# Moving the context's load, transposes and squares from the boundary of two blocks into the feed forward before it

## The reference

```
x = first_block(x, mem, ...)          # per layer: mixer, memory cross attention, feed forward
# second block, layer 0
mod_x, mod_c = silu(c) @ ada_w + ada_b, silu(c_ctx) @ ada_w + ada_b
hx = rmsnorm(x,   n1_g) * (1 + sc1)  + sh1
hc = rmsnorm(ctx, n1_g) * (1 + csc1) + csh1
mx, mc = hybrid_mixer(hx, hc, w_in, ...)

def squared_relu_mlp(h, w1, w2):      # 1024 -> 4096 -> 1024
    a = relu(h @ w1)
    return (a * a) @ w2
```

## Time and profile before

| | |
|---|---|
| median of three runs | 3759.76 us |
| lowest, highest | 3759.74, 3764.34 us |
| the profiled execution | 3764.54 us |
| its span | 3762.7 us |
| PE busy | 3543.3 us, 94% of the span |
| DVE busy | 2017.1 us, 54% |
| ACT busy | 1232.1 us, 33% |
| mean granted clock of PE | 0.951 |

### The profile page before, as it was taken

The page is one execution under the profiler, slowest core; times in us unless marked ns, Lnnn a source line. Parts: engine busy times, 40 slices in busy tenths (PEclk is TensorE's granted clock), DMA queues, the critical chain, the costliest instruction groups (busy, mean ns, idle before and its releaser), DMA issues.

```text
span 3762.7 us, 42305 instructions
## 1 busy us (share of the span) xinstructions
PE 3543.3 (94%) x17448; PEld 2805.7 (75%) x17448; DVE 2017.1 (54%) x3717; ACT 1232.1 (33%) x2053; POOL 212.6 (6%) x302
## 2 busy tenths in 40 slices
PE   7999899999989999998999989999998998879998
PEld 6657678887867678887986557888887885558886
DVE  5565588856654588854126664323235236654344
ACT  4353343234453333233112222332233212134332
POOL 0200000001040000000000001000001000000000
PEclk9999999999999999999999859999999998789999
DMA  4302155522202145533210011212122220112331
GB/s 164 115 12 79 45 168 179 167 91 84 74 27 78 45 157 172 168 119 124 81 57 27 26 38 46 79 57 68 57 66 86 99 68 17 40 45 90 101 91 67
DMA packets 214108, 317.01 MB, mean 84 GB/s; under 512 B 5304, under 2 KB 162618, under 8 KB 212636
## 3 DMA queue, kind: packets, MB, share of 16 engines
q1 hardware_dynamic: 198108, 243.00, 19.9%
q0 software_dynamic: 15808, 71.31, 5.6%
HBM read 300.66 MB, written 14.49 MB: 84 GB/s over the span
## 4 chain that ended last, share of the span: by engine, by line
PE 83%; DVE 11%; ACT 4%; issue 2%; DMA 1%; POOL 0%; SPq 0%; DVEq 0%; ACTq 0%; POOLq 0%
PE ps L94 82%; DVE t L115 5%; ACT t L100 3%; DVE t L107 3%; PE ps L97 1%; DVE t L111 1%; DVE ps L107 0%; DVE ps L115 0%; DVE t L121 0%; DVE t L112 0%; DMA t<-gates_away 0%; DVE t L125 0%; DVE ps L112 0%; DVE t L118 0%; DMA t<-in_mem 0%
## 5 line engine op out<-in xcount | busy, mean ns | idle before, releaser
L94 PE MATMUL ps<-t,t 128*128 128x512 f32 (+7 forms) x17032 | 3486.5, 368 | 193.5 <-DVE t L107 98.1
L94 PEld LDWEIGHTS ps<-t,t 128*128 128x128 f32 (+3 forms) x17032 | 2753.2, 191 | 900.4 <-issue 177.3
L100 ACT ACTIVATE t<-t 128x1024 fp32r<-128x1024 f32 (+6 forms) x1168 | 831.0, 744 | 1226.7 <-PE ps L94 653.5
L107 DVE TENSOR_TENSOR t<-t,t 128x1024 fp32r<-128x1024 f32 (+5 forms) x882 | 781.7, 911 | 708.9 <-ACT t L100 693.5
L100 ACT ACTIVATE t<-ps 128x512 f32<-128x512 f32 (+5 forms) x490 | 248.5, 531 | 1062.7 <-PE ps L94 1027.7
L115 DVE SCALAR_TENSOR_TENSOR t<-t,t,t 128x256 f32<-128x256 f32 (+4 forms) x935 | 438.7, 530 | 7.6 <-ACT t L100 1.2
L107 DVE TENSOR_TENSOR t<-ps,t 128x512 f32<-128x512 f32 (+4 forms) x293 | 187.4, 659 | 248.2 <-PE ps L94 181.8
L115 DVE SCALAR_TENSOR_TENSOR t<-ps,t,t 128x512 f32<-128x512 f32 (+1 forms) x228 | 139.7, 662 | 279.7 <-PE ps L94 259.6
L107 POOL TENSOR_TENSOR t<-t,t 128x64 f32<-128x64 f32 (+1 forms) x196 | 129.3, 684 | 1724.9 <-ACT t L100 1721.6
L118 DVE COPY t<-ps 128x256 f32<-128x256 f32 (+3 forms) x169 | 75.9, 477 | 276.8 <-PE ps L94 256.7
L100 ACT ACTIVATE t<-ps,t 128x512 f32<-128x512 f32 (+3 forms) x106 | 61.6, 582 | 131.9 <-PE ps L94 94.6
(11 more groups left out here) (31 smaller groups left out, 293.3 us busy)
## 6 DMA issues: line engine op xcount, KB each, us to landing
t<-in_w_ff SPq DMA_DIRECT2D x64, 1024.0 KB, 7.6
t<-in_w_mlp SPq DMA_DIRECT2D x64, 1024.0 KB, 5.4
t<-in_ada_w POOLq DMA_DIRECT2D x48, 1024.0 KB, 5.9
t<-in_w_in SPq DMA_DIRECT2D x30, 1024.0 KB, 5.3
t<-in_w_qkv_o SPq DMA_DIRECT2D x12, 1024.0 KB, 5.1
t<-in_w_mem_kv SPq DMA_DIRECT2D x8, 1024.0 KB, 6.0
t<-in_w_mem_q SPq DMA_DIRECT2D x8, 1024.0 KB, 5.1
t<-in_w_mem_o SPq DMA_DIRECT2D x8, 1024.0 KB, 5.1
```

The lines of the kernel that those rows point to most:

```text
L94: return Issued(self, self.e and self.e.matmul(o, l, r, start=start, stop=stop, skip_group_check=True))
L100: return Issued(self, self.e and self.e.activation(o, i, f, **kw))
L107: return Issued(self, self.e and self.e.tensor_tensor(o, a, b, op))
```

## The change

The loading of `ctx_2` moves on SP's queue from the end of the last feed forward to the beginning of the first block's second feed forward, ahead of the load of its second weight block, into a buffer `FF1.CIN` that the stage leaves free; it waits for the last `pv` of the memory attention. In steps 6 to 13 PE transposes one chunk a step into bank 5, behind the step's matmuls, and ACT (even) or DVE (odd) copies it out in the same step. In steps 14 to 21 ACT squares one chunk a step, into the `SQ` buffers, and PE adds it up in bank 5, behind the step's matmuls and ahead of the modulation's. On ACT `context()` stands at the end of each step's work: in an `up` step behind relu, square and copy of both tiles. The norm reads bank 5 in place of 7.

```diff
--- before.py
+++ after.py
@@ -438,11 +438,10 @@
         if with_ada:
             f.ADA = [ar([128, 2048]) for _ in range(2)]
             f.ACC = [ar([128, 2, 256]) for _ in range(2)]
+            f.CIN = [ar([128, D]) for _ in range(2)]
         return f
 
     FF1, FF2 = ff_area(S, True), ff_area(S + C, False)
-    ar = Area(D1)
-    CIN = [ar([128, D]) for _ in range(2)]
     T = S + C
     ar = Area(D1)
     H = Tiles()
@@ -690,9 +689,24 @@
             f1, f2 = ff
             step = [0]
 
+            def context(s):
+
+                if s in range(6, 14):
+                    k = s - 6
+                    opening(5)
+                    pe.wait_ge("ctx_in", 1)
+                    for i in range(2):
+                        ins = pe.transpose(P[5][:, 128 * i:128 * i + 128], tiles.CIN[i][:, 128 * k:128 * k + 128], cst("ident"))
+                    ins.then_inc("ctxT", k)
+                    free[5] = [("ctxT_out", k)]
+                elif s in range(14, 22):
+                    square_sum(("n1_0", 1), 5, C, [s - 14], SQ)
+
             def modulate():
                 s = step[0]
                 step[0] += 1
+                if l == 1:
+                    context(s)
                 if l is None or s > 24 or s == 0:
                     return
                 pe.wait_ge("macc", l, s - 1, 1)
@@ -950,15 +964,6 @@
         memory_attention(1)
 
 
-        pe.wait_ge("ctx_in", 1)
-        for k in range(8):
-            bk = k % 4
-            opening(bk)
-            for i in range(2):
-                ins = pe.transpose(P[bk][:, 128 * i:128 * i + 128], CIN[i][:, 128 * k:128 * k + 128], cst("ident"))
-            ins.then_inc("ctxT", k)
-            free[bk] = [("ctxT_out", k)]
-        square_sum(("n1_0", 1), 7, C, range(8), TMP)
         for l in range(2):
             hybrid_tensor(pe, l, feature, tokens, square_sum, opening, free, normed, project_out, feed_forward)
 
@@ -1320,9 +1325,18 @@
                     for s, (dst, n) in enumerate(streams):
                         square_of(key, s, dst, n, m, ("ev", u.n, m, s))
 
-        def feed_forward(ff, tiles, nkey, key, segs, streams):
+        def feed_forward(ff, tiles, nkey, key, segs, streams, with_context=False):
             f1, f2 = ff
-            at_t = [0]
+            at_t, step = [0], [0]
+
+            def context():
+                s = step[0]
+                step[0] += 1
+                if with_context and s in range(6, 14, 2):
+                    act.wait_ge("ctxT", s - 6)
+                    act.activation(CX[:, s - 6, :], P[5][:, 0:C], ACT.Copy).then_inc("ctxT_out", s - 6)
+                elif with_context and s in range(14, 22):
+                    squares_of(("n1_0", 1), SQ, CX, C, [s - 14], lambda k: ("ctxT_out", k))
 
             def up(j):
                 for u in f1[j]:
@@ -1344,6 +1358,7 @@
                             act.wait_ge("sqr", key, j, t.m, z)
                             act.activation(hid, tb, ACT.Copy).then_inc("hidden_hi", key, j, t.m, z)
                             tmp_free[x] = ("hidden", key, j, t.m, z)
+                    context()
 
             tmp_free = {x: ("nlo", nkey, 7, len(streams) - 1) for x in range(2)}
             up(0)
@@ -1484,7 +1500,7 @@
                       MA.SB, MA.PT, lambda h, part: None)
             project_out(U.mo[l], f"ff{l}", [(X, S)])
             norm(f"ff{l}", [(P[6], S, 0, None)], HR1, [whole(U.mo[l][3])])
-            feed_forward(U.ff[l], FF1, f"ff{l}", "mix1" if l == 0 else "n1_0", [S], [(X, S)])
+            feed_forward(U.ff[l], FF1, f"ff{l}", "mix1" if l == 0 else "n1_0", [S], [(X, S)], l == 1)
 
         memory_attention(0)
 
@@ -1537,11 +1553,6 @@
         memory_attention(1)
 
 
-        for k in range(0, 8, 2):
-            act.wait_ge("ctxT", k)
-            act.wait_ge("pv", ("xat", 1), 3, 1)
-            act.activation(CX[:, k, :], P[k % 4][:, 0:C], ACT.Copy).then_inc("ctxT_out", k)
-        squares_of(("n1_0", 1), TMP, CX, C, range(8), lambda k: ("ctxT_out", k))
         for l in range(2):
             hybrid_scalar(act, l, start, square, sq_free, rs_free, roots, norm, project_out, feed_forward)
 
@@ -1554,7 +1565,7 @@
     def hybrid_scalar(act, l, start, square, sq_free, rs_free, roots, norm, project_out, feed_forward):
         nkey, segs, tasks = f"n1_{l}", segs_of(l), ret_tasks(l)
         hr_free = [whole(U.ff[1][1][7][1]) if l == 0 else whole(U.ff2[0][1][7][1])]
-        norm(nkey, [(P[6], S, 0, lambda k: MOD[l][:, k, 0:1]), (P[7], C, S, lambda k: MOD[l][:, k, 1:2])], HR2, hr_free)
+        norm(nkey, [(P[6], S, 0, lambda k: MOD[l][:, k, 0:1]), (P[5 if l == 0 else 7], C, S, lambda k: MOD[l][:, k, 1:2])], HR2, hr_free)
         for us, dst in ((U.rg[l], H.Q), (U.gg[l], H.K)):
             for u in us:
                 start(u)
@@ -1842,10 +1853,17 @@
             step = [0]
             at_t = [0]
 
+            def context(s):
+                if s in range(7, 14, 2):
+                    dve.wait_ge("ctxT", s - 6)
+                    dve.tensor_copy(CX[:, s - 6, :], P[5][:, 0:C]).then_inc("ctxT_out", s - 6)
+
             def modulate():
 
                 s = step[0]
                 step[0] += 1
+                if l == 1:
+                    context(s)
                 if l is None or s > 24:
                     return
                 if s > 0:
@@ -2114,10 +2132,6 @@
         memory_attention(1)
 
 
-        for k in range(1, 8, 2):
-            dve.wait_ge("ctxT", k)
-            dve.wait_ge("pv", ("xat", 1), 3, 1)
-            dve.tensor_copy(CX[:, k, :], P[k % 4][:, 0:C]).then_inc("ctxT_out", k)
         for l in range(2):
             hybrid_vector(dve, l, start, newton, norm, project_out, feed_forward)
 
@@ -2164,7 +2178,7 @@
             dve.wait_ge("ctxT_out", 6)
             dve.wait_ge("ctxT_out", 7)
         norm(nkey, [(P[6], S, 0, X, lambda k: GM[:, 0, k:k + 1], lambda k: MOD[l][:, k, 0:1]),
-                    (P[7], C, S, CX, lambda k: GM[:, 1, k:k + 1], lambda k: MOD[l][:, k, 1:2])], HR2, hr_free)
+                    (P[5 if l == 0 else 7], C, S, CX, lambda k: GM[:, 1, k:k + 1], lambda k: MOD[l][:, k, 1:2])], HR2, hr_free)
 
         def turned(m):
             x = (H.Q if m < 4 else H.K)[:, m % 4, 0:S]
@@ -2588,10 +2602,12 @@
                     t.then_inc(s_bias[h % 2])
                 else:
                     t.then_inc(s_bias[h % 2], "bias_in", h)
+        before(U.mo[1][3])
+        sp.wait_ge("pv", ("xat", 1), 3, 1)
+        for i in range(2):
+            sp.dma_start(FF1.CIN[i][:, :], A["ctx_2"][0, 128 * i:128 * i + 128, :]).then_inc(s_ctx, "ctx_in", i)
         before(U.ff[1][1][7][1])
         sp.wait_ge(*whole(U.ff[1][1][7][1]))
-        for i in range(2):
-            sp.dma_start(CIN[i][:, :], A["ctx_2"][0, 128 * i:128 * i + 128, :]).then_inc(s_ctx, "ctx_in", i)
         for l in range(2):
             if l == 1:
                 before(U.ff2[0][1][7][1])
```

## The result

| | median us | lowest, highest | runs |
|---|---|---|---|
| before | 3760.83 | 3759.74, 3764.34 | 5 |
| changed | 3797.50 | 3795.70, 3809.29 | 5 |

The changed kernel is slower. The ratio is 1.0094, with a 95% interval of [1.0079, 1.0108]; between the medians are 36.7 us. (The ratios here aren't the quotients of the medians and differ from them by up to 0.001.) In a later comparison, with more runs of before, it was 3795.57 against 3766.16 us, 29.4 us, ratio 1.0075. Forecast were +14.4 us, 3774 us, and a range up to 3781. The profiled execution took 3798.76 us, with a span of 3797.0 us: 34.3 us more than the span of before.

A forecast was written before the change was run, and what follows sets the result against it. PE, busy for 94% of the span, was taken to bound the kernel. The terms -10.2 + 1.8 + 3.5 + 13.8 - 0.5 + 6.0 = +14.4 us, put on the median of 3759.8, gave 3774 us; range 3766 to 3781.

The forecast's parts named there:

- The boundary: Between the last sum and the second block's first projection: 18.87 us shrinks to 8.7 us, a gain of 10.2 us.
- The work on PE: In the feed forward: sixteen transposes add 1.8 us and eight sums 3.5 us, counted in full on PE.
- The waits: Feed forward steps 14, 15, 18 and 19: PE waits 3.45 us each for ACT's square, +13.8 us.
- One sign: In the feed forward: waits of about 3.4 us would stand 48.8 us apart in pairs, steps 14/15 and 18/19.
- The clock behind the waits: After each of four feed forward waits: half-speed clock costs 1.5 us, +6.0 us in all, ends 0 and 12.
- The upper bound: Behind each feed forward wait: a low clock stretch of 5.9 us at half speed costs 3.0 us.
- The sum: Whole kernel: all terms added give +14.4 us, with no change, within 1 us, for the restart at the new boundary.
- A: Rival, feed forward: the waits come but the full clock is held; +8.4 us, 3768.2 us, chance 0.15.
- C: Rival, feed forward: DVE, not PE, sets the pace, so only the boundary's gain is left; -10.2 us, 3749.6, chance 0.03.
- B: Rival, feed forward: ACT's square is early enough in every step, no waits; -5.4 us, 3754.4 us, chance 0.06.
- D: Rival, feed forward: each wait leaves the clock low for 5.9 us, 3.0 us apiece; +20.4 us, 3780.2, chance 0.08.

The follow-up runs named there:

- Transposes alone: Changed kernel with only load, transposes and copies in steps 6 to 13, squares and sums back at the boundary; median 3771.28 us, ratio 1.0006.
- late sums: Changed kernel with PE adding each context square one step later, in steps 15 to 22; median 3768.62 us, ratio 1.0006.
- the filled waits: Changed kernel with four extra result-unused 128x512 matmuls on PE ahead of each of the four waited-for sums; median 3783.04 us, ratio 1.0047.
- the pure delay: Kernel before with 22 extra result-unused 128x512 matmuls on PE in step 28 of the same feed forward; median 3783.69 us, ratio 1.0041.
- three useless matmuls: Kernel with late sums plus three extra result-unused 128x512 matmuls on PE in step 28; median 3754.09 us, ratio 0.9963.

## Why the prediction was right or wrong

**The boundary** was right: 8.71 us, forecast 8.7; gain 10.2 us.

**The work on PE** was right. Transposes alone gave 401.6 us where the same terms gave 401.8, and late sums 400.3 where they gave 401.0.

**The waits** were right in number, place and size: 13.8 us. The order of ACT's rows carried this term, and the idle beside ready work at the boundary said that nothing would overtake. One sign was worded wrongly: the pairs of waits stand 62.2 us apart (1518.10 and 1580.28), not 48.8, since the waits and the low clock lengthen the period between them.

**The clock behind the waits** was under-sized. I took 1.5 us a wait, from the two shorter of three stretches at the low level, and it cost 2.7 (10.8 us over four, by the filled waits; the stage grew by 29.8 us, from 387.5 to 417.3, where the forecast had some 25). The upper bound, 3.0 from the stretch of 5.9 us in the earlier trace rows, was near the truth: the stretches were 6.8, 3.3, 6.1 and 5.9 us. The term was mis-sized by 4.8 us. With it the sum to the first projection is 14.4 + 4.8 = 19.2; measured were 19.6.

**The sum stopped too early.** This is the step that failed. Its last word is "At the new boundary PE idles 8.7 us instead of 8.0 and restarts at the low clock as before: no change, within 1 us". For the restart that held: the projections behind it took 0.4 us more. But the sum has no term for anything behind the restart; the whole second block was put at no change, without a reason. It took 15.5 us more, of which the mixed stage 14.6 and the stretch behind it 1.6. In the mixed stage the clock falls and comes back eight or nine times, and where the first fall lies goes with its length. The 240.1 us in the profile of before were the shortest of five lengths seen, and the forecast took them for granted. Of the 34.3 us between the profiles, 19.6 belong to the edit, its waits and the low clock behind them, and 14.6 to the place at which the mixed stage met the clock; the other rows cancel. The sum to the first projection was short by 5.2 us, which alone would have left the total inside the range (3759.8 + 19.6 = 3779.4): the missing term put it outside.

None of the rivals named this mechanism. A and C were excluded by the clock rows and the four waits; B is what late sums make of the change, and there too the total came out otherwise, 3768.6 where its sum gave 3754.4. D's 3.0 us a wait was nearly reached (2.7), but the total lies 17 us above its 3780.2.

Left open: why the place of the first fall was the same in both profiles of the changed kernel, though the clock's changes stood at other absolute instants in each (first matmul of the feed forward between 1324.15 and 1334.98 us in the profiles), and which groups the timed runs without a profile belonged to. That the groups of runs of one kernel, such as the three of the pure delay, are groups of mixed stage lengths is not shown; the spread of the second layer's stretch can make such groups too. The 36.7 us between the medians are broken down only by way of the two profiles.

## What to carry to other kernels

Before putting work of a second stream into a dense stage, write down for each inserted instruction what stands ahead of it on its producer in the same step, and let the consumer take it one step later; here one step was worth 25.7 us of stage time. Price each wait on PE at its own length plus half of the longest low clock stretch that the trace shows behind a wait of 2 to 4 us; here that gives 3.0 us of clock against the 2.7 measured. A kernel with a long stage that alternates between waits and dense PE work can have several lengths, so a change of a few tenths of a per cent must be read stage by stage, and delays by a few useless matmuls, several of them, help to tell whether a difference belongs to the edit or to the moment.

## What the runs showed of the hardware that I had not expected

Extra work made a kernel faster: three useless matmuls (2.6 us) in place of two (1.7 us) took the median from 3773.69 to 3754.09 us. The length of one stage with unchanged instructions took five values, 240.2, 246.5, 250.3, 251.7 and 254.8 us, each reproduced within 0.12 us where it came more than once; the runs tie them to the place of the granted clock's first fall, and a shift of that fall by 0.4 us (4.26 to 4.67) went with 14.6 us. The version with late sums and three matmuls beats both kernels, 3754.09 us, ratio 0.9963 [0.9945, 0.9980]; 3.4 us of its stage time come from the late sums (402.98 against 406.38), while its mixed stage is just the one that before has. Most of the rest comes from the stretch of the second layer (429.12 against 435.55 us) and from the start, neither of which the edit touches, so any edit ahead of them may lose it again.
